# Query stacks ahead of adaLN loads and sums, and logits, bias and row extremum in one VectorE operation

## The reference, cut to what matters

```python
cond = silu(c); mod = cond @ w_ada + b_ada            # 6 * 1024 values; w_ada is 1024 x 6144
h = rms_norm(x, g1) * (1 + sc1) + sh1
z = h @ w_in                                          # split among four token mixers
# DSA: an indexer (8 heads of 32) scores keys, the top 256 per query are kept
score = sum_h wi[h] * relu(qi[h] . ki * 32**-0.5)
logits = q . k_sel * 64**-0.5 + bias;  p = softmax(logits)
# SWA: window of two chunks, 4 heads of 64, learned sink per head
logits = q . k * 64**-0.5 + bias;  m = max(max(logits), sink)
p = exp(logits - m) / (sum exp(logits - m) + exp(sink - m))
# gMLP and pooling mixers; output projection; ConvGLU with D_FF 2816; final norm
```

## Time and profile before

| | us |
|---|---|
| median of 3 timed runs | 1280.93 (1280.34 to 1284.77) |
| the profiled execution | 1289.74 |
| its span | 1288.0 |
| PE busy | 1214.2 (94%) |
| VectorE busy | 711.4 (55%) |
| ScalarE busy | 577.6 (45%) |
| GpSimd busy | 629.1 (49%) |

### The profile page before, as it was taken

The page is one execution under the profiler, slowest core; times in us unless marked ns, Lnnn a source line. Parts: engine busy times, 40 slices in busy tenths (PEclk is TensorE's granted clock), DMA queues, the critical chain, the costliest instruction groups (busy, mean ns, idle before and its releaser), DMA issues.

```text
span 1288.0 us, 17115 instructions
## 1 busy us (share of the span) xinstructions
PE 1214.2 (94%) x5722; PEld 1003.6 (78%) x5722; DVE 711.4 (55%) x1407; ACT 577.6 (45%) x993; POOL 629.1 (49%) x317
## 2 busy tenths in 40 slices
PE   2797999997999999999999999999999999999997
PEld 1685788875788888888878887888888888888876
DVE  6852778896766798889993434443511112211224
ACT  4244666545663444224421677452544234422443
POOL 1144665793304255445554655434355445544554
PEclk9998999996799999999999999999999999999998
DMA  8456664450112222332224443424222222222234
GB/s 314 156 213 188 209 173 150 154 155 23 50 67 81 82 82 98 98 115 95 93 89 140 134 136 130 147 66 147 82 98 98 98 98 98 97 89 94 96 101 144
DMA packets 58664, 153.91 MB, mean 119 GB/s; under 512 B 6601, under 2 KB 20297, under 8 KB 58609
## 3 DMA queue, kind: packets, MB, share of 16 engines
q1 hardware_dynamic: 47472, 135.12, 31.6%
q10 hardware_dynamic: 11136, 18.09, 4.5%
HBM read 142.66 MB, written 10.52 MB: 119 GB/s over the span
## 4 chain that ended last, share of the span: by engine, by line
PE 44%; issue 24%; POOL 15%; DVE 11%; ACT 3%; DMA 2%; POOLq 0%; ACTq 0%; SPq 0%; DVEq 0%
PE ps L1880 10%; PE ps L1881 10%; PE ps L1883 10%; POOL w_lo L565 10%; DVE unread L1350 4%; POOL act_lo L724 3%; PE ps L2171 2%; PE ps L1904 1%; PE ps L1859 1%; PE ps L1860 1%; PE ps L2150 1%; PE ps L2160 1%; DMA qi_st<-qi_dram 1%; PE ps L1976 1%; PE ps L1864 1%
## 5 line engine op out<-in xcount | busy, mean ns | idle before, releaser
L565 POOL TENSOR_TENSOR w_lo<-w_raw,w_hi 128x1024 fp32r<-128x1024 f32 x148 | 355.0, 2399 | 436.3 <-ACT w_hi L736 436.3
L1880 PE MATMUL ps<-h_hi,w_hi 128*128 128x512 f32 x896 | 355.2, 396 | 0.3 <-POOL w_lo L574 0.3
L1881 PE MATMUL ps<-h_lo,w_hi 128*128 128x512 f32 x896 | 350.4, 391 | 0.0
L1883 PE MATMUL ps<-h_hi,w_lo 128*128 128x512 f32 x896 | 331.5, 390 | 0.0
L736 ACT ACTIVATE w_hi<-w_raw 128x1024 fp32r<-128x1024 f32 x148 | 156.8, 1059 | 335.7 <-PE ps L1883 328.0
L1883 PEld LDWEIGHTS ps<-h_hi,w_lo 128*128 128x128 f32 x896 | 168.5, 188 | 36.0
L1880 PEld LDWEIGHTS ps<-h_hi,w_hi 128*128 128x128 f32 x896 | 169.1, 189 | 35.2 <-POOL w_lo L574 0.7
L1881 PEld LDWEIGHTS ps<-h_lo,w_hi 128*128 128x128 f32 x896 | 169.2, 189 | 32.5
L1752 DVE SCALAR_TENSOR_TENSOR ps<-conv_in,conv_w,ps 128x512 f32<-128x512 f32 x44 | 33.2, 754 | 207.7 <-ACT ps L1148 207.7
L1880 PE MATMUL ps<-act_hi,w_hi 128*128 128x512 f32 x352 | 140.2, 398 | 5.0 <-POOL act_lo L724 2.6
L1883 PE MATMUL ps<-act_hi,w_lo 128*128 128x512 f32 x352 | 137.4, 390 | 0.0
(11 more groups left out here) (255 smaller groups left out, 1862.9 us busy)
## 6 DMA issues: line engine op xcount, KB each, us to landing
w_raw<-in_w SPq DMA_DIRECT2D x173, 512.0 KB, 3.3
w_ada<-in_w_ada SPq DMA_DIRECT2D x48, 512.0 KB, 4.2
x_sb<-in_x SPq DMA_DIRECT2D x4, 1024.0 KB, 9.7
q_st<-qk_dram SPq DMA_DIRECT2D x32, 128.0 KB, 4.1
out<-fin_o ACTq DMA_DIRECT2D x16, 256.0 KB, 2.1
qi_st<-qi_dram ACTq DMA_DIRECT2D x18, 128.0 KB, 6.2
qk_dram<-qk_hi ACTq DMA_DIRECT2D x4, 512.0 KB, 2.7
qk_dram<-qk_lo ACTq DMA_DIRECT2D x4, 512.0 KB, 3.7
```

The lines of the kernel that those rows point to most:

```text
L565: pool.tensor_tensor(r(w_lo[:, slot]), w_raw[:, slot], w_hi[:, slot], ALU.subtract).then_inc(w_lo_ready, 1)
L1880: pe.matmul(ps[:, bank], r(hi_t[:, kk]), r(xh(kk)), start=(i == 0), stop=False)
L1881: pe.matmul(ps[:, bank], r(hi_t[:, kk]), r(xl(kk)), start=False, stop=False)
L1883: mm = pe.matmul(ps[:, bank], r(lo_t[:, kk]), r(xh(kk)), start=False, stop=last_k)
```

## The change

1. ACT issues the stacks of blocks 2 and 3 right behind the index keys, ahead of the loop; in the loop `ada_sums(n - 1)` stands behind `evac(n)`.
2. SP waits for the stacks of block 2 before it loads the first adaLN columns of this stage, and loads the raw weights of unit 6 before that wait. POOL splits the query of unit 3 and makes lo(5) before the first products.
3. The four query units are scaled by 1/8 when they are copied out.
4. In `swa_softmax`, `soft` and `late_soft` one operation for each head makes negated logits with bias and their row minimum (seeded with the negated sink, or with a large constant). The exponentials use scale -1. ACT writes the sink column, and waits for that write. Semaphores `swa_biased` and `dsa_biased` go; their waits take `swa_max` and `dsa_max`.

```diff
             load(4)
             load(5)
-            sp.wait_ge(unit_done, 2)
+            load(N_FIRST + 2)
+            sp.wait_ge(qi_loaded[0], 48)
             for n in range(ADA_UNIT, N_IN):
-                if n >= N_FIRST:
+                if n > N_FIRST:
                     load(n + 2)
...
-            ada_products(ADA_UNIT)
             query_key_lo(U_Q)
             for n in range(N_FIRST, N_IN):
...
                 lo(n + 1)
+                if n == N_FIRST:
+                    ada_products(ADA_UNIT)
                 if n < U_V:
                     query_key_lo(n)
...
-                act.activation(dst, src, f).then_inc(unit_out, 1)
+                if n in (U_Q, U_Q + 1, U_DQ, U_DQ + 1):
+                    act.activation(dst, src, f, scale=HD ** -0.5).then_inc(unit_out, 1)
+                else:
+                    act.activation(dst, src, f).then_inc(unit_out, 1)
...
+            act.wait_ge(qi_stored, 64)
+            for b in TOP_BLOCKS[:2]:
+                stack_queries(b)
             for n in range(N_FIRST, N_IN):
...
-                ada_sums(n - 1)
-                if n == N_FIRST:
-                    act.wait_ge(qi_stored, 64)
-                    for b in TOP_BLOCKS[:2]:
-                        stack_queries(b)
...
                 evac(n)
+                ada_sums(n - 1)
...
             def swa_exps(b, j):
-                act.wait_ge(swa_max, b + 1)
+                act.wait_ge(swa_max, HEADS * b + 2 * j + 1)
+                if j == 0:
+                    act.activation(lg[:, :, 2 * P:2 * P + 1], sinks_neg[:].unsqueeze(2), ACT.Copy).then_inc(swa_sunk, 1)
+                    act.wait_ge(swa_sunk, b + 1)
                 for h in (2 * j, 2 * j + 1):
-                    act.activation(lg[:, h, c0:], lg[:, h, c0:], ACT.Exp, bias=sm_neg_s[:, b % 3, h:h + 1],
+                    act.wait_ge(swa_max, HEADS * b + h + 1)
+                    act.activation(lg[:, h, c0:], lg[:, h, c0:], ACT.Exp, bias=sm_neg_s[:, b % 3, h:h + 1], scale=-1.0,
...
-                dve.tensor_copy(lg[:, :, 2 * P:2 * P + 1], sinks[:].unsqueeze(2))
-                dve.scalar_tensor_tensor(out=lg[:, :, c0:2 * P], in0=src[:, :, c0:], scalar=HD ** -0.5,
-                                         in1=backwards(swa_bias[:, :, 0:2 * P - c0]), op0=ALU.mult, op1=ALU.add
-                                         ).then_inc(swa_biased, 1)
-                dve.wait_ge(swa_biased, b + 1)
-                vlink(dve.tensor_reduce(sm_max_s[:, b % 3], lg[:, :, c0:], AX, ALU.max))
-                dve.tensor_scalar(sm_neg_s[:, b % 3], sm_max_s[:, b % 3], -1.0, None, ALU.mult).then_inc(swa_max, 1)
+                for h in range(HEADS):
+                    dve.tensor_tensor_reduce(out=lg[:, h, c0:2 * P], in0=src[:, h, c0:],
+                                             in1=backwards(swa_bias[:, h, 0:2 * P - c0]), scale=-1.0,
+                                             scalar=sinks_neg[:, h:h + 1], op0=ALU.add, op1=ALU.min,
+                                             accum_out=sm_neg_s[:, b % 3, h:h + 1]).then_inc(swa_max, 1)
...
-                        dve.scalar_tensor_tensor(out=logit4[:, I % 4, 0:n],
...
-                    for e in range(2):
...
-                        vlink(dve.tensor_reduce(sm_max[:, b % 2, hd:hd + 1], logit4[:, I % 4, 0:n], AX, ALU.max))
-                        dve.tensor_scalar(sm_neg[:, b % 2, hd:hd + 1], sm_max[:, b % 2, hd:hd + 1], -1.0, None,
-                                          ALU.mult).then_inc(dsa_max, 1)
+                        dve.tensor_tensor_reduce(out=logit4[:, I % 4, 0:n], in0=ps[:, 4 + e, 0:n], in1=bias, scale=-1.0,
+                                                 scalar=-NO_KEY, op0=ALU.add, op1=ALU.min,
+                                                 accum_out=sm_neg[:, b % 2, hd:hd + 1]).then_inc(dsa_max, 1)
...
```

More of the change, by code:

```diff
@@ L195, in build @@
         sinks = small("sinks", [P, HEADS])
+        sinks_neg = small("sinks_neg", [P, HEADS])
         rel = small("rel", [32, 8])
@@ L217, in build @@
         kept = small("kept", [P, 2 * len(LATE_BLOCKS)])
-        sm_max = small("sm_max", [P, 2, HEADS])
         sm_neg = small("sm_neg", [P, 2, HEADS])
@@ L221, in build @@
         sm_rec = small("sm_rec", [P, 2, HEADS])
-        sm_max_s = small("sm_max_s", [P, 3, HEADS])
         sm_neg_s = small("sm_neg_s", [P, 3, HEADS])
@@ L333, in build @@
         swa_out_ready = sem("swa_out_ready")
-        swa_biased = sem("swa_biased")
+        swa_sunk = sem("swa_sunk")
         dsa_logits_ready = sem("dsa_logits_ready")
-        dsa_biased = sem("dsa_biased")
         dsa_max = sem("dsa_max")
@@ L541, in _ @@
                 if 1 <= k < 15:
-                    sp.wait_ge(dsa_biased, FIRST_LATE + k)
+                    sp.wait_ge(dsa_max, FIRST_LATE + k)
                     bias_slice(FIRST_LATE + k + 1)
@@ L660, in masked_bias @@
                 if I >= 10:
-                    pool.wait_ge(dsa_biased, I - 1)
+                    pool.wait_ge(dsa_max, I - 1)
                 pool.tensor_tensor(bias_e[:, I % 2, 0:P * (b + 1)], backwards(bias_0[:, hd, 0:P * (b + 1)]),
@@ L959, in exps @@
                         act.wait_ge(dsa_max, I + 1)
-                        act.activation(lg, lg, ACT.Exp, bias=sm_neg[:, b % 2, hd:hd + 1],
+                        act.activation(lg, lg, ACT.Exp, bias=sm_neg[:, b % 2, hd:hd + 1], scale=-1.0,
                                        accum_out=sm_sum[:, b % 2, hd:hd + 1]).then_inc(dsa_exp, 1)
@@ L1072, in _ @@
                             act.wait_ge(gmlp_out, 4)
-                            act.wait_ge(swa_biased, NBLK)
+                            act.wait_ge(swa_max, HEADS * NBLK)
                             act.dma_start(x2_of[0][:], a["x"].rearrange("(k p) s -> p k s", p=P)[:, :, 0:HALF]
@@ L1546, in gmlp_output @@
                                          op0=ALU.add, op1=ALU.mult).then_inc(gmlp_out, 1)
+            vlink(dve.tensor_scalar(sinks_neg[:], sinks[:], -1.0, None, ALU.mult))
             swa_softmax(0)
@@ L1574, in soft @@
                             bias = backwards(bias_0[:, hd, 0:n])
-                        dve.scalar_tensor_tensor(out=logit4[:, I % 4, 0:n],
-                                                 in0=ps[:, 4 + e, 0:n],
-                                                 scalar=HD ** -0.5, in1=bias,
-                                                 op0=ALU.mult, op1=ALU.add).then_inc(dsa_biased, 1)
-                    for e in range(2):
-                        hd = 2 * (i % 2) + e
-                        I = HEADS * b + hd
-                        dve.wait_ge(dsa_biased, I + 1)
-                        vlink(dve.tensor_reduce(sm_max[:, b % 2, hd:hd + 1], logit4[:, I % 4, 0:n], AX, ALU.max))
-                        dve.tensor_scalar(sm_neg[:, b % 2, hd:hd + 1], sm_max[:, b % 2, hd:hd + 1], -1.0, None,
-                                          ALU.mult).then_inc(dsa_max, 1)
+                        dve.tensor_tensor_reduce(out=logit4[:, I % 4, 0:n], in0=ps[:, 4 + e, 0:n], in1=bias, scale=-1.0,
+                                                 scalar=-NO_KEY, op0=ALU.add, op1=ALU.min,
+                                                 accum_out=sm_neg[:, b % 2, hd:hd + 1]).then_inc(dsa_max, 1)
                 def final_norm(hh, g):
@@ L1598, in late_soft @@
                     dve.wait_ge(bias_and_mask, I - 7)
[L1599 to L1605, removed]
+                    dve.tensor_tensor_reduce(out=lg, in0=ps[:, 2:4].rearrange("p a c -> p (a c)")[:, 0:n],
+                                             in1=backwards(bias_m[:, I % 2, 0:n]), scale=-1.0,
+                                             scalar=-NO_KEY, op0=ALU.add, op1=ALU.min,
+                                             accum_out=sm_neg[:, b % 2, hd:hd + 1]).then_inc(dsa_max, 1)
                 def late_out(b):
@@ L1951, in swa_logits @@
                 if b >= 1:
-                    pe.wait_ge(swa_biased, b)
+                    pe.wait_ge(swa_max, HEADS * b)
                 for h in (0, 2, 1, 3):
@@ L2007, in gating @@
                     pe.wait_ge(consts_set, 4)
-                    pe.wait_ge(swa_biased, NBLK)
+                    pe.wait_ge(swa_max, HEADS * NBLK)
                     pe.wait_ge(vn_ready, 1)
@@ L2023, in logits @@
                     if I > 0:
-                        pe.wait_ge(dsa_biased, I)
+                        pe.wait_ge(dsa_max, I)
                     pe.wait_ge(k_loaded, 32 * HEADS)
@@ L2092, in _ @@
                     if h == 0 and i == 4:
-                        pe.wait_ge(dsa_biased, FIRST_LATE)
+                        pe.wait_ge(dsa_max, FIRST_LATE)
                     if i == 6 or h == 1:
```

## The result

The changed kernel takes 1313.74 us (median of four runs, 1309.44 to 1316.37) against 1282.85 for the kernel before, a ratio of 1.0232 [1.0187, 1.0278]. The direction was right; 1295 was too low, and 1313.7 lies above the range. Four more runs of the changed kernel, beside 13 of the kernel before, gave 1309.82 against 1284.83, 1.0174 [1.0129, 1.022]: 25 to 31 us lost, where I had worked out 14.

The account below looks back on a forecast made before the run. PE's own list was taken to bound 119 to 235 and 690 to 880 us, low-weight margins to decide this change. 15.9 + 2 + 0.8 - 3.2 = +15.5, taken as +14, gave 1304 profiled, 1295 timed; range 1280 to 1303.

Parts of the forecast that it names:

- my 15.5: Sum of the forecast's terms over the whole kernel: 15.9 + 2 + 0.8 - 3.2 us slower, taken as +14.
- Stacks earlier: Start of the in-projection's dots: dot 0 gains 9.2 us, dot 4 is held, unit 6 starts 4.1 us earlier.
- Sums behind the copy: In-projection from unit 7: later sums delay the low parts PE needs; unit 18 ends 15.9 us late.
- the 4.1 of head start: At unit 6 of the in-projection: start at 114.9 against 119.05, 4.1 us gained by earlier stacks.
- I add 2 us, bounds 0 and 4: In-projection: PE running slow after two long holes of 4.6 and 7.9 us, charged 2 us.
- Into attention, +0.8: Passage into attention: sums ahead of ACT's gate copies, plus the sink column, cost 0.8 us (-0.6 to +2).
- Together -3.2: Attention: one operation per head shortens PE's wait by 1.2 us and 340 to 365 by 2, saving 3.2.
- the clock comes back in attention: Rival, 22%: PE's shorter wait at 317 restores the clock in attention; steps cost 8 us less, 1287.
- The ring: In-projection's adaLN ring through POOL's list delays unit starts; the rival that it does not bind, 1273 to 1276, had 10%.
- Slow clock: Rival, 10%, shared with a fused operation at two cycles a column: slow after every hole, 3 to 8 us more, 1298 to 1303.
- the likeliest case: The forecast's main outcome for the whole kernel: 1295 us, 1289 to 1301 alone, chance 58%.

Follow-up runs that it names:

- pooling_later: The changed kernel with POOL's two pooling steps of turn 16 moved behind the low part of unit 18; 1310.71 us, 1.0213 of the kernel before.
- sums_back: The changed kernel with the sums back in the middle of the unit, early stacks and fused operations kept; 1283.76 us against 1283.37 for the kernel before, 0.9996.
- before_again: The kernel before, unchanged, for a second profile and more runs; median 1281.91 us against 1284.83 for other runs of the same code, profiled span 1280.1.
- low_first: The changed kernel with POOL's products of turn n - 1 behind the low part and the query-key low part of turn n; 1300.92 us, 1.0141.
- stacks_first_fused: stacks_first with the attention part (one VectorE operation per head) added; 1278.03 us, 0.9962 of the kernel before.
- fused_only: The kernel before with only the attention part of the change, in-projection as before; 1286.45 us against 1283.37, 1.0015.
- low_first_2: The changed kernel with POOL's products of turn n - 1 directly behind turn n's low part, ahead of the query-key low part; 1285.31 us against 1282.43, 1.0027.
- stacks_first: The kernel before with only ACT's first turn changed: query stacks ahead of the first sums, these behind the copy; 1278.02 us against 1282.43, 0.9958.

## Why the prediction was wrong in size

Against the first profile of before, spans differ by 19.7 us; against the second, which stands at the median, by 1307.7 - 1280.1 = 27.6. This second difference is the one to hold beside my 15.5: attention's start 23.7 (306.21 - 282.56), attention 2.1 (86.96 - 84.86), the fold 1.5 (8.65 - 7.12), the rest 0.3. The 2.1 need not be the change's: with the old operations attention took 84.9, 86.6, 89.3 and 93.4 us in four profiles, with the new ones 86.9 to 88.3 in seven of eight (93.5 in pooling_later, with its wait of 8.80).

- **Stacks earlier: right in place, in part by luck.** Dot 0 at 96.5 came at 96.42; dot 4 held to 107.9 came at 108.45; unit 6 at 114.9 came at 115.51. But SP issued the columns at 93.61, not at 95.4, and POOL had them at 100.47, 6.9 us later instead of 4.35; the two errors nearly cancel:

```profile
100.47 4.70 POOL L606 TENSOR_TENSOR w_ada<-w_ada,cond 128x1024 f32<-128x1024 f32 x2 [6.96 <-DMA w_ada<-in_w_ada]
```

- **Sums behind the copy: right in mechanism, place and nearly in size.** From unit 6 to attention the changed kernel takes 190.7 us, the first profile of before 162.4, so 28.3 more. Of that 18.3 are waits for low parts, 2.1 the wait for v behind the sums (2.36, where sums_back has 0.29), 0.8 a dot. That is 21.2 us of holes where I had 20.0 (15.9 and the 4.1 of head start). The first of them was off by the most: unit 7 at 133.2 instead of 128.8. Unit 5 ended 2.9 us later than I had it (115.5 instead of 112.6), since its second half ran mostly at 1.2 GHz behind dot 4 (0.63 us a matmul until 112.7); and I had left out that stacks of the next block (115.72, 2.0 us of issue) stand ahead of its copy. The 5 us stayed to unit 16.
- **"I add 2 us, bounds 0 and 4", for the slow clock: the term that failed.** What is left of the 28.3 us is 7. Unit 16 takes 13.7 us and unit 18 13.1 instead of 10.9, and their windows show 0.62 and 0.63; in unit 7 the matmuls take 0.63 us instead of 0.39 from 133.9 to 137.4. I had charged 2 us for two long holes; three brought a slow stretch: some 1.6 us behind 3.45 (unit 7), 2.8 behind 2.36 and 1.98 with 0.7 us of work between (unit 16), 2.2 behind 6.61 (unit 18). pooling_later shows for unit 18 that the stretch goes with the hole. Holes of 1.91, 2.39 and 1.27 us ahead of units 9, 11 and 13 brought none (granted clock 1.00 behind them). The fold's 1.5 us are slow clock too (0.82 behind 393.17), but not behind a longer hole: the last waits ahead of it are 0.82 and 0.54 us, as in before_again, where it runs at 1.00:

```profile
393.17 8.90 PE L2105 MATMUL ps<-diag_y,y 128*128 128x128 f32 x64
```

  The fold takes 8.7 to 9.0 us in seven of the eight profiles with one operation a head (7.36 in low_first) and 7.36 in all four profiles with the old operations. It goes with the attention part, then; why is not settled.
- **Into attention, +0.8: about right.** The waits for the gate copies grew from 1.2 to 2.8 us.
- **"Together -3.2", for one operation a head: the other term that failed.** The operation has its estimated 0.41 us, and a block saves 1.0 of VectorE as I said; of that no gain reaches the median, in two pairs of kernels (1.0015 with its interval above, and 1278.03 beside 1278.02). I read its path from 340 to 365 off an execution in which PE had just come back from 1.2 GHz. What the one shrinking wait gives (3.63 to 2.56 here), longer waits elsewhere and the slower fold take back, as stacks_first_fused shows. fused_only's 3 us above the median beside it are within its interval: its ten runs lie at clocks of 0.976 to 0.981 and those of before beside them at 0.973 to 0.985, and what sets this was not shown.
- **The rivals.** That the clock comes back in attention because VectorE's wait shrinks is not borne out: in before_again the wait is 3.6 us as before, and the clock does come back (0.93). In the stretch that answers to 315 to 340 us, four profiles with the old operations show 0.52, 0.93, 0.88 and 0.74, and those with the new ones 0.80 (0.73 in fused_only). My base was the slowest of the four, and that hid 8 us of the loss in the first pair of profiles. The ring did bind. Slow clock, to which I gave 10% together with a slower operation at 3 to 8 us, is what the runs show, though behind the long holes and not behind every one; its price beside the likeliest case was right, the chance was not. My range ended there, at 1303, and slow clock, lost saving and longer holes together went past it.

On the fused operation the Trainium skill (Vector Engine (DVE) Microarchitecture Reference, Points that are easy to get wrong) halves the rate for two fp32 sources in SBUF. The new operation has one of its two in PSUM, and from 256 to 1024 columns its rows go from 481 to 1221 ns, about 1 ns a column (groups of VectorE in the changed kernel):

```profile
L1512 DVE CUSTOM_DVE_ANT_0 logit<-ps,swa_bias,sinks_neg 128x256 f32<-128x256 f32 x28 | 11.9, 481 | 12.2 <-PE ps L1949 10.9 <-issue 1.1 <-DVE score L1459 0.3
```
```profile
L1596 DVE CUSTOM_DVE_ANT_0 logit_late<-ps,bias_m 128x1024 f32<-128x1024 f32 x4 | 4.9, 1221 | 2.1 <-PE ps L2144 1.8 <-DVE sum L1782 0.3
```

The plain operation that it replaces takes 1215 ns for 1024 columns, so there is no half rate here; the case that the rule names, both sources in SBUF, no new operation of this change has. That the attention part came to nothing, as the rule would have it, has other grounds: the operation is as fast as I had it.

## What to carry to other kernels

When work is moved to a later place on one engine, follow the whole ring that it closes through the other queues, and look for the item that stands between the late work and a wait of the bounding engine; exchanging the two in the list (low_first_2, 1.0027 of the kernel before) gave back nearly as much as undoing the move (sums_back, 0.9996). Read the granted clock of a stage from more than one execution before a saving is read off that stage, and charge the longer holes on TensorE with the slow matmuls behind them, 1.6 to 2.8 us each here. An operation that replaces one wide pass by one for each head can also free its PSUM banks later; time saved on an engine that does not end the stage is no gain.

## What had not been expected of the hardware

A DMA issue that is moved by a few us can decide how long its neighbours take: six query stacks landed after a median of 8.4 us with 1.5 MB of loads issued within 1.5 us of them, and after 3.3 with these loads seven us later (3.2 in stacks_first, with the loads at 100.4). The same code, on the same chip, spread over 1279.9 to 1290.6 us in 19 runs, with a mean granted clock of 0.985 in the shortest and 0.975 in the longest.
